# Packing TensorE's small products and taking the first expert's tokens by a product, in a decoder layer (S5, sparse attention, mixture of experts) on one core

## The reference, cut to what matters

```python
h = layer_norm(x)
u, q, k, v, q_idx, k_idx, w_idx, gate_pre = split(h @ w_in)
# A: S5. 32 groups x 64 complex states, diagonal, scanned over positions
bu = einsum('blgp,gnp->blgn', u, b_bar); states = scan(a_bar, bu)
y = gelu(Re(einsum('blgn,gpn->blgp', states, c)) + d_skip * u); val, gate = split(y @ w_glu); y_ssm = val * sigmoid(gate)
# B: for each query the 128 best keys by an index score, then attention over them with distance penalties
score = einsum('bqh,bhqs->bqs', w_idx, relu(einsum('bqhd,bsd->bhqs', q_idx, k_idx)))     # 8 heads of 64
y_att = softmax(q k^T - slope * dist, over the chosen keys) @ v @ w_attn_proj            # 8 heads of 64
h = layer_norm(ALPHA * h + (g_ssm * y_ssm + g_att * y_att) @ w_o)
# experts: top 4 of 32; blocks of tokens of one expert
hdn = xb @ w_up[e] + b_up[e]; act = clamped_swiglu(hdn); y = (act @ w_down[e] + b_down[e]) * gate
out = layer_norm(ALPHA * h + sum of y over a token's four experts)
```

## Time and profile before

| | |
|---|---|
| median of 3 runs (lowest, highest) | 1841.83 us (1840.55, 1843.05) |
| the profiled execution, own time | 1839.94 us |
| its span, first to last instruction | 1838.2 us |
| PE busy | 1696.1 us, 92% |
| DVE busy | 1519.6 us, 83% |
| ACT busy | 1081.0 us, 59% |
| POOL busy | 524.9 us, 29% |
| chain that ended last | PE 77%, DVE 14%, issue 3%, ACT 3% |
| mean granted TensorE clock | 0.952 of 2.4 GHz |

### The profile page before, as it was taken

The page is one execution under the profiler, slowest core; times in us unless marked ns, Lnnn a source line. Parts: engine busy times, 40 slices in busy tenths (PEclk is TensorE's granted clock), DMA queues, the critical chain, the costliest instruction groups (busy, mean ns, idle before and its releaser), DMA issues.

```text
span 1838.2 us, 22681 instructions
## 1 busy us (share of the span) xinstructions
PE 1696.1 (92%) x7227; PEld 1139.8 (62%) x7227; DVE 1519.6 (83%) x1709; ACT 1081.0 (59%) x1032; POOL 524.9 (29%) x310
## 2 busy tenths in 40 slices
PE   3989998989998589999999999999999999999992
PEld 2333356766657257777777777777777777777761
DVE  6899927944566779999999999999999999999994
ACT  4333113345444247777777777777777777777770
POOL 4655113356053271212122121212212221121220
PEclk9999989999999589999999999999999999999996
DMA  6110121121031669999999999999999999999963
GB/s 193 46 46 13 41 85 46 47 92 47 16 120 67 237 235 332 378 360 368 365 369 363 366 383 358 364 372 363 361 371 377 359 363 372 368 362 370 381 267 106
DMA packets 93084, 465.44 MB, mean 253 GB/s; under 512 B 22404, under 2 KB 22520, under 8 KB 43800
## 3 DMA queue, kind: packets, MB, share of 16 engines
q1 hardware_dynamic: 81776, 443.90, 63.6%
q0 software_dynamic: 9424, 16.86, 4.0%
q10 hardware_dynamic: 1848, 4.24, 0.6%
HBM read 454.81 MB, written 18.92 MB: 258 GB/s over the span
## 4 chain that ended last, share of the span: by engine, by line
PE 77%; DVE 14%; issue 3%; ACT 3%; DMA 1%; POOL 1%; ACTq 0%; DVEq 0%; POOLq 0%
PE ps L1696 19%; PE ps L1698 19%; PE ps L1697 19%; PE ps L1682 3%; PE ps L1441 2%; PE ps L1704 2%; PE ps L1436 2%; PE ps L1422 2%; DVE scr L1112 1%; DVE top L1111 1%; DVE scr L1062 1%; PE ps L1552 1%; PE ps L1430 1%; DVE scr L1061 1%; PE ps L1571 1%
## 5 line engine op out<-in xcount | busy, mean ns | idle before, releaser
L1190 DVE TENSOR_TENSOR w_lo<-raw,w_hi 128x2048 fp32r<-128x2048 f32 x384 | 874.5, 2288 | 82.4 <-ACT w_hi L846 82.3
L846 ACT ACTIVATE w_hi<-raw 128x2048 fp32r<-128x2048 f32 x384 | 736.9, 1920 | 242.5 <-PE ps L1698 242.5
L1696 PE MATMUL ps<-w_hi,x_hi 128*96 128x512 f32 x1024 | 415.1, 405 | 0.0
L1698 PE MATMUL ps<-w_lo,x_hi 128*96 128x512 f32 x1024 | 403.8, 394 | 0.0
L1697 PE MATMUL ps<-w_hi,x_lo 128*96 128x512 f32 x1024 | 403.5, 394 | 0.0
L624 POOL DMA_INDIRECT gate_now<-gate_rows,row_now x32 | 80.3, 2510 | 468.4 <-DVE tok_out L1318 447.8
L1698 PEld LDWEIGHTS ps<-w_lo,x_hi 128*96 128x96 f32 x1024 | 165.9, 162 | 71.3
L1696 PE MATMUL ps<-w_hi,a_hi 128*96 128x512 f32 x512 | 204.6, 400 | 5.7 <-DVE a_lo L1289 5.7
L1696 PEld LDWEIGHTS ps<-w_hi,x_hi 128*96 128x96 f32 x1024 | 168.7, 165 | 66.2 <-issue 0.4
L1697 PEld LDWEIGHTS ps<-w_hi,x_lo 128*96 128x96 f32 x1024 | 166.4, 163 | 64.8
L1697 PE MATMUL ps<-w_hi,a_lo 128*96 128x512 f32 x512 | 201.4, 393 | 0.0
(11 more groups left out here) (311 smaller groups left out, 2303.8 us busy)
## 6 DMA issues: line engine op xcount, KB each, us to landing
raw<-in_w_up SPq DMA_DIRECT2D x256, 1024.0 KB, 8.5
raw<-in_w_down SPq DMA_DIRECT2D x128, 1024.0 KB, 7.2
ring<-in_w_in SPq DMA_DIRECT2D x9, 2048.0 KB, 7.7
ring<-in_w_glu SPq DMA_DIRECT2D x4, 1024.0 KB, 6.3
ring<-in_w_o SPq DMA_DIRECT2D x2, 2048.0 KB, 13.1
h<-in_x SPq DMA_DIRECT2D x4, 512.0 KB, 4.8
ring<-in_w_attn_proj SPq DMA_DIRECT2D x1, 2048.0 KB, 7.9
h_rows<-h ACTq DMA_DIRECT2D x4, 512.0 KB
```

The costliest lines, as they stand in the source:

```text
L846: s.activation(hi_of(c)[:, :], raw_of(c), ACT.Copy).then_inc(s_hi, 1)
L1190: d.tensor_tensor(lo_of(c)[:, :], raw_of(c), hi_of(c)[:, :], ALU.subtract).then_inc(s_lo, 1)
L1696: mm(o, xh, hi_of(c)[:, col], start=start, stop=False)
L1698: return mm(o, xh, lo_of(c)[:, col], start=False, stop=stop)
```

## The change

It has these parts. (a) `ymm(q)` now makes the C products of four `j` on the four column groups, in turn, and stands at three places of the tile loop and once behind the index weights (L1509); the `bu` are spread wider; `w_st` has five buffers, the two new ones being `far` and `gb`, so the load of `gb` waits for the last `ymm`. (b) Index dots and `qk` are issued in pairs of two heads, into four and three PSUM banks. (c) The second normalisation makes two passes instead of three over a row. (d) The up biases are kept as two fp32r parts (64 rows) instead of three bf16 parts (96 rows); ACT and POOL have fewer copies for it between the tiles. (e) The tokens of expert 0 come from a product of a one-hot tile `in_first` with the positions; the last `write_first` comes after the first gather; the tables, half of the gated biases (`sums`), and the further addresses are done later, the last of them at the end of blocks 0 to 3; the write of `sum_rows` moves from SP to POOL. ACT makes one `hi` fewer before it takes the last tile's transposes.

```diff
-        w_st = [scr[:, 8:12], scr[:, 12:16], ring[:, 5, 1536:3584]...]
+        w_st = [scr[:, 8:12], scr[:, 12:16], ring[:, 5, 1536:3584]...,
+                far[:, :, :], gb[:, :, :].rearrange("p r (k t) -> p (r k) t", k=2)]
...
-            def ymm(p):
-                q = p // 2
-                pe.wait_ge(s_st, 2 * p + 2)
-                if p % 2 == 0 and q > 1:
+            def ymm(q):
+                pe.wait_ge(s_st, 4 * q + 4)
+                if q > 1:
                     pe.wait_ge(s_yfree, q - 1)
                 for k, r in enumerate((0, 2, 1, 1)):
-                    for j in (2 * p, 2 * p + 1):
+                    for j in range(4 * q, 4 * q + 4):
                         rows = slice(32 * (j % 4), 32 * (j % 4) + 32)
-                        ins = mm(ps[5 - q % 2][rows, :], cblk[:, r, j, :], w_st[j % 3][:, k, :], ...)
+                        ins = mm(ps[5 - q % 2][rows, :], cblk[:, r, j, :], w_st[j % 5][:, k, :], ...)
...
+            bu_at = {1: 1, 4: 2, 7: 3, 9: 4, 12: 5, 14: 6, 17: 7}
+            y_at = {6: 0, 11: 1, 16: 2}
...
-                if i % 2 == 0 and 1 <= i // 2 <= SJ // 2:
-                    ymm(i // 2 - 1)
-                if i % 2 == 1 and i // 2 + 1 < SJ // 2:
-                    bu(i // 2 + 1)
+                if i in y_at:
+                    ymm(y_at[i])
+                if i in bu_at:
+                    bu(bu_at[i])
...
             ins.then_inc(s_wi, 1)
+            ymm(3)
...
-            for i in range(24):
+            for i in range(0, 24, 2):
...
-                if i >= 2:
-                    pe.wait_ge(s_relu, i - 1)
-                mm(ps[5 + i % 2][:, 0:NQT[t]], qiT[rows, hh // 2, ...], kiT[rows, 0:NQT[t]], ...).then_inc(s_dot, 1)
-                for _ in range(gates_after(i)):
+                if i >= 4:
+                    pe.wait_ge(s_relu, i - 2)
+                for j in (i, i + 1):
+                    rows, pair = slice(64 * (j % 2), 64 * (j % 2) + 64), j % HEADS // 2
+                    ins = mm(ps[DOT_BANKS[j % 4]][:, 0:NQT[t]], qiT[rows, pair, ...], kiT[rows, 0:NQT[t]], ...)
+                ins.then_inc(s_dot, 1)
+                for _ in range(gates_after(i + 1)):
...
             def qk(i):
-                mm(ps[5 + i % 2]..., qT[rows, ...], kT[rows, ...]).then_inc(s_qk, 1)
+                for j in (i, i + 1):
+                    t, hh = STEPS[j]
+                    rows = slice(64 * (hh % 2), 64 * (hh % 2) + 64)
+                    ins = mm(ps[QK_BANKS[j % 3]][:, 0:NQT[t]], qT[rows, ...], kT[rows, ...], ...)
+                ins.then_inc(s_qk, 1)
...
             for i in range(len(STEPS) + 3):
-                if i < len(STEPS):
+                if i < len(STEPS) and i % 2 == 0:
                     qk(i)
...
-                step(norm(h[:, t, :], TT + t + 1, step))
-                step(d.tensor_tensor(h[:, t, :], h[:, t, :], gb[:, 0, :], ALU.mult))
-                d.tensor_tensor(h[:, t, :], h[:, t, :], gb[:, 1, :], ALU.add).then_inc(s_h1, 1)
+                step(d.scalar_tensor_tensor(h[:, t, :], h[:, t, :], mvx[:, t, 0:1], gb[:, 0, :], ALU.subtract, ALU.mult))
+                d.scalar_tensor_tensor(h[:, t, :], h[:, t, :], rsx[:, t, 1:2], gb[:, 1, :], ALU.mult, ALU.add)\
+                    .then_inc(s_h1, 1)
...
-                        mm(ps[n][0:BLK, :], pick[:, :], bias3[:, 512 * n:512 * n + 512], start=True, stop=False)
+                        mm(ps[n][0:BLK, :], pick[:, :], b_up[:, 512 * n:512 * n + 512], start=True, stop=False)
...
+                d.tensor_scalar(in_first[:, t, :], tcol[:, 0:BLK], pos[:, t, 0:1], chosen[:, t, 0:1], ALU.is_equal,
+                                ALU.mult).then_inc(s_inf, 1)
...
+            for t in range(TT):
+                ins = mm(ps[0][0:BLK, 64:65], in_first[:, t, :], qpos[:, t:t + 1], start=t == 0, stop=t == TT - 1)
+            ins.then_inc(s_tok0, 1)
...
-            dve.wait_ge(s_slots, 16)
-            dve.wait_ge(s_h1row, 16 * TT)
-            d.tensor_scalar(tok_now[:, :], slots[:, 0:1], 2, None, ALU.arith_shift_right).then_inc(s_tnow, 1)
+            dve.wait_ge(s_tok0, 1)
+            d.tensor_copy(tok_now[:, :], ps[0][0:BLK, 64:65]).then_inc(s_tnow, 1)
+            dve.wait_ge(s_cnt, 1)
+            step(d.tensor_copy(cnt, ps[2][:, 0:NE]))
+            pick_expert(0)
+            lo(-1, 5)
+            dve.wait_ge(s_h1row, 16 * TT)
+            sums(0)
+            sums(1)
             lo(-1, 6)
...
             for half in range(2):
                 T_lo(x_lo, x_hi, half, half, 6 + half)
+            tables()
+            final = dve.value_load(etab_i[0:1, NB:NB + 1], min_val=NE - 1, max_val=NB - 2)
+            dve.wait_ge(s_slots, 16)
             next_token(1)
...
             for p in range(8):
                 up_part(-1, p + 4, p)
+                if p == 2:
+                    gated_biases(2)
+                if p == 5:
+                    pe.wait_ge(s_gbf, 6)
+                    gated_biases(3)
...
-            dve.wait_ge(s_slots_m, 16)
...
+            for i in range(TT):
+                blk(i)
+                if i >= TT - MORE_TILES:
+                    more_addresses(i)
```

More of the change, by code:

```diff
@@ L426, in _ @@
             sp.wait_ge(s_mix, 8)
-            for r in range(3):
+            for r in range(2):
                 sp.dma_start(braw_b[NE * r:NE * r + NE, :], a["b_up"][0]).then_inc(s_bias, 16)
@@ L515, in _ @@
             step(g.iota(code[:, :], pattern=[[P * TOPK, TT], [1, TOPK]], base=0, channel_multiplier=TOPK))
-            step(g.memset(eye96[:, :], 0.0))
-            for r in range(3):
-                step(g.affine_select(out=eye96[:, :], in_=eye96[:, :], compare_op=ALU.not_equal, fill=1.0,
+            step(g.memset(eye2[:, :], 0.0))
+            for r in range(2):
+                step(g.affine_select(out=eye2[:, :], in_=eye2[:, :], compare_op=ALU.not_equal, fill=1.0,
                                      base=-NE * r, pattern=[[-1, NE]], channel_multiplier=1))
@@ L580, in _ @@
                 pool.wait_ge(s_wolo, n + 1)
[L582 to L585, removed]
+            second = slice(NE, 2 * NE)
+            pool.wait_ge(s_bhi, 1)
+            g.tensor_tensor(b_up[second, :], braw_b[second, :], b_up_hi[second, :], ALU.subtract).then_inc(s_blo, 1)
+            pool.wait_ge(s_blo, 1)
             g.memset(xg[:, :], 0.0).then_inc(s_one, 1)
@@ L655, in _, with write_more @@
                 rows_out(i)
+            def write_more(t):
+                pool.wait_ge(s_adr_m, t + 1)
+                for c in range(TOPK * t - FIRST, TOPK * (t + 1) - FIRST):
+                    g.indirect_dma_start(more_list, bass.IndirectOffsetOnAxis(ap=more_i[:, c:c + 1], axis=0),
+                                         code[:, FIRST + c:FIRST + c + 1], None, bounds_check=BLK * BTAIL - 1,
+                                         oob_is_err=False).then_inc(s_scat_m, 16)
+            for i in range(2 * TT):
+                blk(i)
+                if i >= TT and i - TT >= TT - MORE_TILES:
+                    write_more(i - TT)
+            pool.wait_ge(s_scat_m, 16 * MORE_TILES * TOPK)
+            g.dma_start(slots[:, NE:], more_list.rearrange("(p b) o -> p (b o)", p=BLK)).then_inc(s_slots_m, 16)
+            with pool.Fori(2 * TT, final) as i:
+                blk(i)
             gates_in(final)
@@ L952, in _ @@
             step(d.memset(half_pi[:, :], TWO_PI / 4))
-            def norm(row, n, step):
-                for r in range(2):
-                    step(d.bn_stats(stats[:, r, :], row[:, 512 * r:512 * r + 512]))
-                d.bn_aggr(mv[:, :], stats[:, :, :]).then_inc(s_var, 1)
-                dve.wait_ge(s_rstd, n)
-                step(d.reciprocal(rstd[:, 1:2], rstd[:, 0:1]))
-                dve.wait_ge(s_var, n)
-                return d.tensor_scalar(row, row, mv[:, 0:1], rstd[:, 1:2], ALU.subtract, ALU.mult)
             def measure(t):
@@ L1206, in _ @@
                 if t == TT - 1:
-                    for c in range(4, 6):
-                        lo(-1, c)
+                    lo(-1, 4)
                 dve.wait_ge(s_lgt, t + 1)
@@ L1656, in _ @@
             place(TT - 1)
+            pe.wait_ge(s_inf, TT)
+            for t in range(TT):
+                ins = mm(ps[0][0:BLK, 64:65], in_first[:, t, :], qpos[:, t:t + 1], start=t == 0, stop=t == TT - 1)
+            ins.then_inc(s_tok0, 1)
             for b in range(TT):
```

225 lines of the change are left out of this document (111 added, 114 removed).

## The result

The changed kernel takes 1882.13 us (median of 4 runs, 1874.66 to 1884.45), against 1842.35 us (1840.55 to 1843.05) for the kernel before. The ratio is 1.0208, with a 95% interval from 1.0185 to 1.0231: slower by 2.1%, where 2.2% faster had been forecast, and outside the range. The profiled execution took 1883.4 us, with a mean granted clock of 0.936 against 0.952 before.

A forecast was written before the change was run, and what follows sets the result against it. PE was taken to bound the expert loop, DVE S5 up to 184.7 us and PE behind it, PE to lead attention. Terms summed to -40.2 us, giving 1801.6 us (0.64 for 1790 to 1812); whole range 1784 to 1822.

The forecast's parts named there:

- three signs of being wrong: Prediction wrong if `hT_lo` starts later than 255 us, attention is not under 105 us, or a block takes over 36.2.
- (a) The four column groups: S5 C products: a `ymm` of four `j` takes the same 3.56 us as one of two.
- the first rival: S5: the four column groups do not run beside each other, 14 of 21.3 us go, 1816 us; chance 0.12.
- (a) Where it counts: S5 around the seventh `bu`: PE's idle time holds 10.5 us more work, `hT_lo` starts at 248.4; -21.3 us.
- (b) Dots: Gate stage, index dots in pairs: PE no longer waits for `relus` between them; -2 us, bounds 0 and -6.
- (b) Logits: Attention stage, `qk` in pairs: PE's 23.4 us halve to 11.7, 1 us taken off; -11 us, bounds -5 and -18.
- (c), (d) and (e) up to the first bias product: Routing: second normalisation and copies -3.4 us, first tokens 15.2 earlier; -18.6 in all to block -1's first bias product.
- (d) Biases in the loop: Expert loop: fp32r costs 0.06 and 64 rows 0.2 us, x 32; +8.3 us, lower bound +2.
- the fourth rival: Expert loop: bias products run at plain float32 pace, 81 us instead of 8.3, 1875 us; chance 0.03.
- (e) Further addresses: Expert loop: DVE's 3.76 us of addresses leave a few tenths in each of four blocks; +0.5 us, bounds 0 and +4.
- The sum: Whole kernel: -21.3 - 2 - 11 - 3.4 - 11.3 + 8.3 + 0.5 = -40.2 us.
- The rivals: Column groups serial 0.12; waits elsewhere, 1813 us, 0.10; more gain, 1789 to 1796, 0.08; float32 pace 0.03.

The follow-up runs named there:

- Run 2: Changed kernel with the four-`j` C products kept, `bu` back at its old places, last four ahead of the index weights: 1866.51 us, 1.0127 of the kernel before.
- run 5: Run 4's kernel, with ACT copying tile j + 1 ahead of the trigonometric values of j from j = 6 on: 1823.15 us, 0.9909 of the kernel before.
- run 7: Kernel before the change, its bf16 bias products reading 64 of the 96 rows, third part of each bias left out: 1849.98 us, ratio 1.0057.
- run 1: Changed kernel with the S5 order of before (C products of two `j`, old `bu` places): 1863.46 us, 1.0112 of the kernel before.
- run 11: Run 9's kernel with the attention stage's GLU tiles issued at odd steps: 1792.27 us, 0.9742 of the kernel before.
- run 12: Changed kernel with all five edits: run 9's three, last four ahead of the index weights, GLU tiles at odd steps: 1794.76 us, 0.975 of the kernel before.
- runs 6 and 7: 6: run 4's kernel with fp32r bias operands padded to 96 rows, 1833.13 us, 0.9964 of the kernel before; run 7 has its own line.
- Run 4: Changed kernel with POOL's four indirect writes of the further list moved behind the gather of their block: 1848.41 us, 1.0031 of the kernel before.
- run 9: Changed kernel with three edits: POOL's writes behind the gather, ACT's takes first from j = 6, 96-row bias operands: 1810.03 us, 0.982 of the kernel before.

## Why the prediction was wrong

Two of its three signs of being wrong came: `hT_lo` at 284.6, later than 255, and an attention stage of 110.2 us, not under 105. The third did not, since a block takes 36.08 us where none waits.

**(a) The four column groups: right.** 32 records in 3.62 us on the chain, against 16 in 3.56; the first rival is out. The Trainium skill, page "TensorE: Matmul & The Clock Gate", section on measured speedup against the span model, had three column tiles at 2.38 times; by the estimate from it a four would have taken 4.4 us. The row decides: one behind the other, 32 records of 0.44 us would be 14.1 us (an estimate from the earlier trace rows), so four column groups ran at 3.9 times here.

**(a) Where it counts: wrong.** The step that failed is "3 tiles are done earlier (21.2 us) and 5 old `ymm` (17.8) have become 2 (7.1): 10.5 us more work before the trigger. PE's 14.4 us of idle time there hold it." It counted PE's time and not whether PE may start. A tile waits for ACT's copy of the tile two before it, and that copy stands behind `trigs`, which waits for DVE. In the kernel before this never showed, because `bu` stood early enough. With `bu` three tiles later, the seventh came at 203.0 and not at 184.7. Run 2 (early `bu`) gives 18.5 us back and run 5 (ACT's order) 23.8. With that tie gone the rest of the step is nearly right: from the seventh `bu` to the end of the last four 63.6 us in run 5, forecast 57.5. Of the 6 us, 1.9 are the first `bu` (3.78 instead of 1.92), 2.2 the tile behind it and 2.8 the last four (6.37 instead of 3.57), less 0.3 for the index weights. These were slower by the granted clock, 0.84 in this stretch, which the sum had left out.

**(b) Dots:** -4.5 instead of -2, right in kind. The twelve traces with dots in pairs have 118.7 to 120.1 us here; run 7 and the kernel before have 123.9.

**(b) Logits:** forecast -11, measured -2.8. The price of the operation was right: 25.4 us became 13.0 in run 1, and there the stage is 10.8 shorter. The step that failed is the silent one, that the rest of PE's work keeps its pace. An estimate from the clocks of the windows: at 0.90 for 110 us, about 22 us (2 x 0.10 x 110) pass at 1.2 GHz instead of 2.4, against 7 before (2 x 0.03 x 113); half of the other 15 is lost, 7.5 us of the missing 8.2. What makes the clock fall in one run and not in the other isn't settled: code and waits of the stage are the same. That PE's gaps have to do with it is shown by run 11 only so far as an order with fewer of them had 0.98 and 0.97 (run 12).

**(c), (d) and (e) up to the first bias product:** -17.7 against -18.6. Up to the fourth tile's logits on DVE it is -3.9 (forecast -3.4), from the positions to the first bias product -14.1 (forecast -15.2): the four products started 1.4 us after the tokens, behind transposes and a copy on ACT. Neither part was run alone. The tokens took 2.15 us instead of 2.2, the four gated biases 7.2 instead of 7.1. In block -1 +3.7 (34.5 to 38.2), forecast +3.9.

**(d) Biases in the loop:** the mechanism was right, the size off. The term "0.06 + 0.2 = 0.26, x 32" is 0.08 for the type and 0.33 for the rows, 0.41 x 30 = 12.3 us instead of 8.3. The Trainium skill, page "TensorEngine Tiling (Array Packing)", section Key Properties, says that a change of the tiling mode drains TensorE; runs 6 and 7 agree, since 64 rows cost 0.33 us a block in either type and 96 rows cost nothing. The float32 pace, the fourth rival, didn't come.

**(e) Further addresses: wrong, and the dearest step.** "They take 3.76 us at most ...; DVE idles 58.2 us in 800 ... +0.5, bounds 0 and +4." It priced what DVE does and left out what the addresses are for: sixteen indirect writes on POOL, some 2.9 us each from one to the next, four of them ahead of a gather. The diff has POOL's loop among what was moved; the sum looked at POOL's queue for the first list and not for this one. 80% idle on POOL was no cover: a gather 11.4 us later made PE wait 7.43 us, so it had only 4.0 us to spare there. Four such waits are 25.1 us, and PE's lower clock behind them 10.6 more, 35.7 in all. Run 4 shows that the place in the list did it.

**The sum.** -40.2, with S5 as it came (36.2 more) and the writes (35.2 more) is +31.2; the attention stage adds 8.2 and the biases 4.0, together +43.4, and the small terms cancel. The rivals looked at prices and at waits in other stages. None looked at the order in ACT's list in S5 or in POOL's list in the loop, and these two decided.

## What to carry to other kernels

When an instruction is moved later in one engine's list, ask which other lists wait for it, and whether an engine with idle time may start at all: an order such as "first the values for the next step, then the copy that frees the buffer" ties the two engines on either side of it. When work is put off, follow it to the last queue that it passes: the slack that counts is that of the instruction standing behind it, not the idle share of the engine. And read the granted clock of every stage with the idle time of PE: here the same attention code took 102.2 us at 0.98 and 110.2 at 0.90, and moving the GLU tiles to the steps without a pair of logits (run 11 against run 9) took 13.0 us off the stage, where the pairs alone had taken 2.8.

## What the runs showed of the hardware

Four column groups of 32 columns ran beside each other at full pace, 3.62 us for 32 records of 512 columns. One section of 64 rows among products of 128 rows costs 0.33 us, one of 96 rows nothing that shows, in bf16 and in fp32r alike. Sixteen scattered writes of a column each slowed neither the weights' transfers nor the gathers beside them (363 GB/s in the window of run 4, as in the loop before); only their place in POOL's list did. A wait of PE costs more than itself: four waits of 25.1 us came with 10.6 us of slower matmuls behind them, 0.42 us apart instead of 0.23. And the clock of the attention stage differed between kernels with the same code there, by 8.0 us between run 1 and the changed kernel; executions of one kernel differed by 12 us in run 9. What sets it is open.
